# Expert layers of a two-block network: routing weights from one product per token, with GpSimd taking part

## The reference, cut to what matters

```
s = einsum('thpk,pnk->thpn', q, sub_keys); s_top, i_top = top_k(s, 16)
cand = s_top[:, :, 0, :, None] + s_top[:, :, 1, None, :]
g_top, pos = top_k(cand, 16); expert = i_top0 * 128 + i_top1 at pos
g = softmax(g_top)
act = gelu(einsum('thkd,td->thk', u[expert], x))
out = einsum('thk,thkd->td', g * act, v[expert])
```

## Time and profile before

| what | value |
|---|---|
| median of 3 runs | 2693.94 us |
| lowest and highest run | 2690.03 and 2698.76 us |
| span of the profiled execution | 2688.2 us |
| expert layers' up tiles with routing steps | about 401.6 to 663 and 1401 to 1663 us |
| granted clock of PE in these stretches | 1.00 |

### The profile page before, as it was taken

The page is one execution under the profiler, slowest core; times in us unless marked ns, Lnnn a source line. Parts: engine busy times, 40 slices in busy tenths (PEclk is TensorE's granted clock), DMA queues, the critical chain, the costliest instruction groups (busy, mean ns, idle before and its releaser), DMA issues.

```text
span 2688.2 us, 48883 instructions
## 1 busy us (share of the span) xinstructions
PE 2605.5 (97%) x17304; PEld 2387.0 (89%) x17304; DVE 1996.2 (74%) x3791; ACT 1506.0 (56%) x2602; POOL 346.1 (13%) x190
## 2 busy tenths in 40 slices
PE   6999999999999999999999999999999999998998
PEld 6779999999888888889999999888888889887997
DVE  6768957888887876669867888666666686677766
ACT  4455557766565556555557766665554544463443
POOL 4007600000000002617500000000000101002000
PEclk9999999999999999999999999999999999999999
DMA  6844564444788874424664444555555345442553
GB/s 243 282 137 164 197 228 149 142 143 148 266 279 272 280 264 145 149 94 167 204 213 143 148 142 150 195 191 192 195 187 187 108 176 188 165 164 96 187 188 133
DMA packets 134733, 490.88 MB, mean 183 GB/s; under 512 B 15520, under 2 KB 15608, under 8 KB 134288
## 3 DMA queue, kind: packets, MB, share of 16 engines
q1 hardware_dynamic: 131904, 480.31, 52.6%
q0 software_dynamic: 2640, 8.02, 0.9%
HBM read 487.21 MB, written 1.06 MB: 182 GB/s over the span
## 4 chain that ended last, share of the span: by engine, by line
PE 87%; DVE 6%; ACT 2%; DMA 2%; issue 1%; POOL 0%; SPq 0%; DVEq 0%; ACTq 0%
PE ps L224 78%; PE ps L1308 4%; DMA weight_ring<-in_stream 2%; ACT weight_split L239 1%; PE ps L641 1%; DVE weight_split L248 1%; DVE arena L633 1%; ACT arena L396 1%; PE ps L2473 1%; PE ps L1280 1%; POOL weight_split L248 0%; DVE arena L1909 0%; PE ps L389 0%; DVE arena L1913 0%; PE ps L662 0%
## 5 line engine op out<-in xcount | busy, mean ns | idle before, releaser
L224 PE MATMUL ps<-hT_split,weight_split 128*128 128x256 f32 x9792 | 1234.3, 285 | 9.8 <-DVE hT_split L421 4.6
L224 PEld LDWEIGHTS ps<-hT_split,weight_split 128*128 128x128 f32 x9792 | 1196.2, 192 | 20.1 <-issue 13.8
L248 DVE TENSOR_TENSOR weight_split<-weight_ring,weight_split 128x1024 fp32r<-128x1024 f32 x674 | 823.5, 1223 | 403.0 <-ACT weight_split L239 400.4
L239 ACT ACTIVATE weight_split<-weight_ring 128x1024 fp32r<-128x1024 f32 x800 | 848.2, 1061 | 259.7 <-PE ps L224 167.8
L224 PE MATMUL ps<-weight_split,hidden_split 128*128 128x512 f32 x3948 | 914.8, 391 | 7.6 <-DVE hidden_split L1574 4.0
L224 PEld LDWEIGHTS ps<-weight_split,hidden_split 128*128 128x128 f32 x3948 | 736.4, 188 | 160.9 <-issue 8.0
L248 POOL TENSOR_TENSOR weight_split<-weight_ring,weight_split 128x1024 fp32r<-128x1024 f32 x126 | 306.2, 2433 | 410.5 <-ACT weight_split L239 410.2
L1404 ACT ACTIVATE hidden_split<-arena 128x256 fp32r<-128x256 f32 (+1 forms) x256 | 176.3, 689 | 249.0 <-PE ps L224 248.5
L1396 ACT ACTIVATE arena<-ps 128x256 f32<-128x256 f32 (+18 forms) x248 | 126.9, 512 | 133.5 <-PE ps L224 133.5
L224 PE MATMUL ps<-weight_split,hT_split 128*128 128x512 f32 x660 | 159.1, 396 | 9.0 <-DVE weight_split L248 4.7
L1574 DVE TENSOR_TENSOR hidden_split<-arena,hidden_split 128x256 fp32r<-128x256 f32 x256 | 161.2, 630 | 0.0
(11 more groups left out here) (357 smaller groups left out, 1765.7 us busy)
## 6 DMA issues: line engine op xcount, KB each, us to landing
weight_ring<-in_stream SPq DMA_DIRECT2D x912, 512.0 KB, 3.3
x<-in_x SPq DMA_DIRECT2D x1, 1024.0 KB, 5.0
arena<-mlstm_m_rows POOLq DMA_DIRECT2D x1, 1024.0 KB, 6.7
arena<-in_ln_mix_g POOLq DMA_DIRECT2D x2, 512.0 KB, 4.8
arena<-in_ln_mix_b POOLq DMA_DIRECT2D x2, 512.0 KB, 6.2
arena<-in_ln_ffn_g POOLq DMA_DIRECT2D x2, 512.0 KB, 4.6
arena<-in_ln_ffn_b POOLq DMA_DIRECT2D x2, 512.0 KB, 6.3
out<-x SPq DMA_DIRECT2D x2, 512.0 KB, 2.6
```

The costliest lines, as they stand in the source:

```text
L224: mm = pe.matmul(out_, stationary(s_part), moving(m_part), start=start and n == 0, stop=stop and n == 2, skip_group_check=True)
L239: act.activation(wsplit[:, n % SPLITS, HIGH, :], ring[:, slot(POS[n]), :], ACT.Copy).then_inc(high_ready, 1)
L248: eng.tensor_tensor(w[:, REST, :], ring[:, slot(POS[n]), :], w[:, HIGH, :].bitcast(fp32), ALU.subtract).then_inc(split_ready, 1)
```

## The change

The four one-hots of a step are shared out anew, and PE gets another product:
- POOL `places_i` makes the four plain one-hots of i (no weight), as fp32r, one instruction a token, two steps ahead. Its first two steps wait for the columns and for the last use of the buffer (mod_ready).
- The weights g are split once a layer into HIGH and REST (`pr_gain`, ACT and DVE `gains_rest`). DVE `places_j` makes for every token a pair of one-hots of j, one weighted by HIGH, one by REST: one instruction of 2x128 elements with two SBUF tensors and one scalar, two tokens at a time, into six slots.
- PE takes one fp32r product of 128x256 a token: the plain one-hot stationary, the pair moving. The two halves of the result, in two pairs of PSUM banks, have to be added.
- ACT `high_out` copies the HIGH halves of a step (512 elements) to SBUF (`pr_w`). DVE `summed` adds the REST halves: the weights of done tiles into `pr_w`, those of later tiles into `acts_late`.
- POOL `weigh` multiplies the activations of done tiles by `pr_w`, all in SBUF.
- ACT's `keep` and `places_j`, DVE's `places_i` and `weigh` are gone.
- The scratch space of software transfers is set to 8192.

The diff, cut to its core:

```diff
+        pr_gain = sbuf("routing_gains_split", [128, 2, T], fp32r)
+        pr_w = sbuf("routing_weights", [128, 2, 4, 128])
...
+            def places_i(q):
+                if q >= 2:
+                    pool.wait_ge(pr_built, STEPS * l + q - 1)
+                for a in range(STEP):
+                    step = pool.tensor_scalar(pr_ohi[:, q % 2, a], iota[:], pr_cols[:, 0, STEP * q + a:STEP * q + a + 1], None, ALU.is_equal)
+                step.then_inc(pr_ohi_r, 1)
+
+            def weigh(q):
+                w, tokens = pr_w[:, q % 2], slice(STEP * q, STEP * q + STEP)
+                pool.wait_ge(pr_summed, STEPS * l + q + 1)
+                pool.wait_ge(activated_ready, 128 * l + STEP_AT[q])
+                early, late = acts_early[:, tokens, :], acts_late[:, tokens, 0:STEP_AT[q] - EARLY]
+                pool.tensor_tensor(early, early, w[:, :, 0:EARLY], ALU.mult)
+                pool.tensor_tensor(late, late, w[:, :, EARLY:STEP_AT[q]], ALU.mult).then_inc(pr_routed, 1)
+
+            pool.wait_ge(pr_cols_out, 2 * (l + 1))
+            pool.wait_ge(mod_ready, 14 if l else 6)
+            places_i(0)
+            places_i(1)
+            for q in range(STEPS):
+                weigh(q)
+                if q + 2 < STEPS:
+                    places_i(q + 2)
...
             def routing(q):
                 pe.wait_ge(pr_ohi_r, STEPS * l + q + 1)
+                pe.wait_ge(pr_ohj_r, 2 * (STEPS * l + q + 1))
+                if q >= 2:
+                    pe.wait_ge(pr_summed, STEPS * l + q - 1)
                 for a in range(STEP):
-                    mm = pe.matmul(ps[:, q % 3, 128 * a:128 * a + 128], pr_ohi[:, q % 2, a, :], pr_ohj[:, q % 3, a, :].bitcast(fp32),
-                                   start=True, stop=True)
+                    mm = pe.matmul(ps[:, 2 * (q % 2) + a // 2, 256 * (a % 2):256 * (a % 2) + 256], pr_ohi[:, q % 2, a, :],
+                                   pr_ohj[:, (STEP * q + a) % J_SLOTS].rearrange("p k j -> p (k j)"), start=True, stop=True)
...
+            def high_out(q):
+                act.wait_ge(pr_built, STEPS * l + q + 1)
+                if q >= 2:
+                    act.wait_ge(pr_routed, STEPS * l + q - 1)
+                    act.wait_ge(pr_kept, STEPS * l + q - 1)
+                act.activation(pr_w[:, q % 2], step_weights(q, HIGH), ACT.Copy).then_inc(pr_high_out, 1)
...
             for j in range(128):
                 if j - 1 in STEP_AT:
-                    keep(with_step(j - 1))
-                if j + 1 in STEP_AT:
-                    places_j(with_step(j + 1))
+                    high_out(with_step(j - 1))
...
+            def summed(q):
+                w, low, tokens = pr_w[:, q % 2], step_weights(q, REST), slice(STEP * q, STEP * q + STEP)
+                dve.wait_ge(pr_high_out, STEPS * l + q + 1)
+                dve.tensor_tensor(w[:, :, 0:STEP_AT[q]], low[:, :, 0:STEP_AT[q]], w[:, :, 0:STEP_AT[q]], ALU.add).then_inc(pr_summed, 1)
+                dve.tensor_tensor(acts_late[:, tokens, STEP_AT[q] - EARLY:], low[:, :, STEP_AT[q]:], w[:, :, STEP_AT[q]:], ALU.add).then_inc(pr_kept, 1)
...
+            def places_j(q, pair):
+                n = q - 1 + pair
+                if n >= 1:
+                    dve.wait_ge(pr_built, STEPS * l + n)
+                for a in (2 * pair, 2 * pair + 1):
+                    t = STEP * q + a
+                    step = dve.scalar_tensor_tensor(out=pr_ohj[:, t % J_SLOTS], in0=iotas(2), scalar=pr_cols[:, 1, t:t + 1],
+                                                    in1=pr_gain[:, :, t:t + 1].bitcast(fp32).broadcast_to([128, 2, 128]), op0=ALU.is_equal, op1=ALU.mult)
+                step.then_inc(pr_ohj_r, 1)
...
             for j in range(HEAD, 129):
-                if j - 1 in STEP_AT:
-                    weigh(with_step(j - 1))
+                if j in STEP_AT:
+                    places_j(with_step(j), 1)
                 if j + 1 in STEP_AT:
                     if with_step(j + 1) == 0:
-                        dve.wait_ge(pr_cols_out, 2 * (l + 1))
-                    places_i(with_step(j + 1))
+                        gains_rest()
+                    places_j(with_step(j + 1), 0)
                 if j + 2 < 131:
                     up_rest(j + 2)
                 if j == FIRST_STEP - 2:
                     mod_out_dve(row, 7)
+                if j - 1 in STEP_AT:
+                    summed(with_step(j - 1))
                 if j - 1 >= FIRST_STEP:
                     weigh_tile(j - 1)
-                if j + 1 in STEP_AT:
-                    places_j(with_step(j + 1))
```

More of the change, by code:

```diff
@@ L126, in build @@
             pass
+        with nc.sbuf_tensor("below_places", [128, ROUTE + 768], fp32), nc.sbuf_tensor("places_i", [128, 2, 4, 128], fp32r) as pr_ohi:
+            pass
         arena = sbuf("arena", [128, EDGE])
+        pr_gain = sbuf("routing_gains_split", [128, 2, T], fp32r)
+        pr_w = sbuf("routing_weights", [128, 2, 4, 128])
         ps = ctx.enter_context(nc.psum_tensor("ps", [128, 8, 512], fp32))
@@ L1225, in build, with step_weights @@
         pr_sum = pr(2, TB * 8)
-        pr_cols = edge_a.rearrange("p (n t) -> p n t", n=3)
-        STEP, ACT_J = 4, 2
+        pr_cols = edge_a[:, 0:2 * T].rearrange("p (n t) -> p n t", n=2)
+        STEP, J_SLOTS = 4, 6
         STEPS = T // STEP
         assert len(STEP_AT) == STEPS and EARLY < FIRST_STEP
-        pr_ohi = edge_b.rearrange("p (n a i) -> p n a i", n=2, a=STEP)
-        pr_ohj = hidden[:].rearrange("p n a t -> p (n a t)").rearrange("p (n a i) -> p n a i", n=3, a=STEP)
+        pr_ohj = hidden[:].rearrange("p n a t -> p (n a t)").rearrange("p (n k j) -> p n k j", n=J_SLOTS, k=2)
         (pr_par, pr_q_out, pr_scored, pr_s_out, pr_topped, pr_chosen, pr_exp_in, pr_exp, pr_cols_t, pr_cols_out,
-         pr_ohi_r, pr_distance, pr_ohj_act, pr_ohj_dve, pr_built, pr_routed, pr_kept, pr_weighted) = (sem("peer_" + s) for s in (
+         pr_gain_r, pr_ohi_r, pr_ohj_r, pr_built, pr_high_out, pr_summed, pr_routed, pr_kept, pr_weighted) = (sem("peer_" + s) for s in (
              "params_in", "q_out", "scored", "scores_out", "topped", "chosen", "exp_in_ready", "exp_ready", "cols_turned", "cols_out",
-             "onehots_i_ready", "places_distance_ready", "onehots_j_act_ready", "onehots_j_dve_ready", "routing_built", "done_tiles_weighted",
+             "gains_split", "onehots_i_ready", "onehots_j_pair_ready", "routing_built", "routing_high_out", "routing_summed", "done_tiles_weighted",
              "routing_kept", "tile_weighted"))
-        def step_weights(q):
-            return ps[:, q % 3, :].rearrange("p (a j) -> p a j", a=STEP)
+        def step_weights(q, part):
+            b = 2 * (q % 2)
+            return ps[:, b:b + 2, :].rearrange("p b (a k j) -> p (b a) k j", a=2, k=2)[:, :, part, :]
         def with_step(j):
@@ L1409, in hidden_first @@
                 hidden_top(j)
-            def keep(q):
-                act.wait_ge(pr_routed, STEPS * l + q + 1)
-                act.activation(acts_late[:, STEP * q:STEP * q + STEP, STEP_AT[q] - EARLY:], step_weights(q)[:, :, STEP_AT[q]:], ACT.Copy).then_inc(pr_kept, 1)
-            def places_j(q):
-                if q >= 3:
-                    act.wait_ge(pr_built, STEPS * l + q - 2)
-                for a in range(ACT_J):
-                    step = act.activation(pr_ohj[:, q % 3, a, :], iota[:], ACT.Abs, scale=-1.0, bias=pr_cols[:, 1, STEP * q + a:STEP * q + a + 1])
-                step.then_inc(pr_distance, 1)
-                act.wait_ge(pr_distance, STEPS * l + q + 1)
-                near = pr_ohj[:, q % 3, 0:ACT_J]
-                act.activation(near, near.bitcast(fp32), ACT.Relu, scale=-1.0, bias=1.0).then_inc(pr_ohj_act, 1)
+            def high_out(q):
[4 more added lines that the diff above has]
+                act.activation(pr_w[:, q % 2], step_weights(q, HIGH), ACT.Copy).then_inc(pr_high_out, 1)
             def exps():
@@ L1536, in up_rest, with gains_rest @@
                     ada_dve((104 if l else 40) + (j - HEAD) // 2, edge_b)
-            def weigh(q):
-                g, tokens = step_weights(q), slice(STEP * q, STEP * q + STEP)
-                dve.wait_ge(pr_built, STEPS * l + q + 1)
-                dve.wait_ge(activated_ready, 128 * l + STEP_AT[q])
-                early, late = acts_early[:, tokens, :], acts_late[:, tokens, 0:STEP_AT[q] - EARLY]
-                dve.tensor_tensor(early, early, g[:, :, 0:EARLY], ALU.mult)
-                dve.tensor_tensor(late, late, g[:, :, EARLY:STEP_AT[q]], ALU.mult).then_inc(pr_routed, 1)
+            def gains_rest():
+                dve.wait_ge(pr_cols_out, 2 * (l + 1))
+                dve.tensor_tensor(pr_gain[:, REST, :], ps[:, 3, 0:T], pr_gain[:, HIGH, :].bitcast(fp32), ALU.subtract).then_inc(pr_gain_r, 1)
+                dve.wait_ge(pr_gain_r, l + 1)
+            def summed(q):
[3 more added lines that the diff above has]
```

(1 more changed line is left out.)

22 lines of the change are left out of this document (3 added, 19 removed).

## The result

The changed kernel takes 2799.56 us (median, 2797.47 to 2801.51) against 2691.99 us of the kernel before beside it: a ratio of 1.0404, 95% interval 1.0387 to 1.0422, about 108 us **slower**. The sign was forecast and the time lies inside the stated range, but the forecast of 33 us more is a third of what came.

A forecast was written before the change was run, and what follows sets the result against it. PE bounds the routing stretch before; after, DVE with POOL's turns: 3.70 + 0.53 = 4.23 us a step, a group 31.0 against 29.2, over 18.3 groups 33 us more, 2727 us. Range of 8 in 10: 2650 to 2840.

The forecast's parts named there:

- the term of 0.53 us a step: In DVE's step tile: POOL's 2.50 us less 0.97 beside PSUM reads and 1.00 of hidden start-up leaves 0.53 added.
- POOL alone would fit within 3.36: POOL's work in a routing step, 2.50 us, low end 1.62, was to fit within PE's step tile of 3.36 us.
- PE: Routing product on PE falls from 0.88 to 0.48 us, a step tile from 3.76 to 3.36; 51 us if PE stayed the bound.
- ACT: ACT in the routing stretch loses work and gains one 512-element PSUM copy, up to 1.06 us: nothing on the path.
- DVE's list: DVE's work in a step tile without POOL: 1.13 + 4 x 0.40 + 0.68 + 0.29 = 3.70 us, a group 27.3.
- two instructions with 512 elements together make 0.68: DVE's two sums of a step: 0.08 us fixed each and 1.02 ns an element, together 0.68 us.
- second case: PE and DVE alone count, POOL's small instructions slipping in between DVE's: 34 us less, 2660 us; chance 0.27.
- POOL's price: POOL's four one-hots at 0.38 us each plus two weighing products at 0.98 us: 2.50 us a step.
- The weighing: POOL's two products of a step, mean 352 elements together: 0.82 to 0.98 us, 0.98 taken.
- Taking turns: DVE instructions reading two SBUF tensors and POOL's reading SBUF exclude each other: 33 us more, 2727 us; chance 0.53.
- My sum with DVE as the bound: DVE's step tile 3.70 + 0.53 = 4.23 us, its group 31.0 us against PE's 29.2 before: 33 us more.
- third case: Turns without hidden start-ups, or POOL dearer than its one row says: 161 us more, 2855 us; chance 0.20.

The follow-up runs named there:

- first experiment: Changed kernel with POOL's one-hots of i one element wide from the third step on and both weighing products one element each: 2686.08 us, ratio 0.9982.
- third experiment: Changed kernel with DVE's pairs reading the numbers from PSUM and its REST parts subtracting a PSUM bank (wrong values), so no shared reads: 2692.51 us, ratio 1.0001.
- the edit of 2: Changed kernel with the row of numbers copied once a layer to PSUM, so DVE's pairs read only one SBUF tensor: 2734.96 us, ratio 1.0154.

## Why the prediction was right or wrong

The forecast was 33 us more, the result 108. **The step that failed is the term of 0.53 us a step, POOL's time put into DVE's list, with POOL's own waiting put at nothing ("POOL alone would fit within 3.36").** In its place the runs show POOL as the bound: a list of 3.3 us a step without company, and on top about 1.2 us of waiting for its turn on average; in the step shown both make 4.83 us. The parts, one by one:

- **PE: right.** Where PE had to wait, it is 562.66 - 562.09 = 0.57 us from the start of the four passes to the next tile's products; where it had not, 0.47, and step tiles follow each other by 3.35 us (first experiment: routing products at 403.12 and 406.47, the tile's own at 403.59), as worked out. The gain of 0.40 us a step was real and could not be collected.
- **ACT: right.** It is busy for 107.3 us of the stretch, and the sum waits for its copy for 3.5 us in all (DVE L1565).
- **DVE's list: too short by 0.18 us a step.** The term that is off is "two instructions with 512 elements together make 0.68"; it is 0.86 (third experiment), and the 0.18 is a wait that the change adds and that I did not see, 0.10 of it between the two records: `weigh_tile` now waits for a sum of its own engine that stands right in front of it, where ACT's copy had been early. The pairs (0.39 against 0.40) were right. With 3.88 a group takes 7 x 3.88 + 1.42 = 28.6 us against 29.2: the case without turns is about 11 us less, and not 34. The first experiment gave 6 us less, the third no difference; the two halves of its REST part make 0.06 us a step, 8 us, of that. A slip in the prediction's second case, 24.9 for what is 27.3 - 8 x 0.29 = 25.0, is worth 1 to 2 us.
- **POOL's price: too low by 0.8 us a step.** "A one-hot: 0.20 us by the memset's line, 0.38 by the product's. I take 0.38." It is 0.58 start to start. The product's line was drawn through one point, with the memset's fixed part; the fixed part of this instruction is 0.28. The weighing was nearer (0.98 forecast, 1.0 to 1.1 measured). What the prediction calls a product of 1024 on POOL is the subtraction of L248; the true products are shorter in their fixed part than the one-hots, 0.19 us with one element in the first experiment (L1288, median 191 ns). POOL's own list is 4 x 0.58 + 1.0 = 3.3 us a step, not 2.50.
- **Taking turns: right as a mechanism, wrong in who pays.** I put POOL's time into DVE's list and let POOL keep its own price. In fact DVE lost 554 - 477 = 77 ns on a pair, 0.3 us a step, and POOL 906 - 603 = 303 ns on a one-hot, 1.2 us a step. With a list of its own of 3.3 us that makes POOL's 4.5 to 5 us the pace, and PE waits for one-hots rather than for split tiles, as I had said. My sum with DVE as the bound (4.23 us a step) gave a third of the loss. Price and waiting were both needed: the third experiment has the full price and no loss, and a list of 2.50 with 1.2 of waiting would take 3.7 us (an estimate), less than DVE's 3.88 and 0.3.
- **The range held in part by luck.** With the measured prices in it the same sum reads 3.32 - 0.97 - 1.00 = 1.35 us a step, DVE's tile 3.88 + 1.35 = 5.23 and a group 38.0 against 29.2: 161 us more, too much by half. Prices that were too low and the wrong engine made up for each other in part.
- **The rivals.** The second case, that small instructions would slip in between, is refuted by the third experiment beside the changed kernel. Granted clock and loss do not go together: with the edit of 2 the clock over the run is 0.992, within the 0.990 to 0.997 of the kernel before, and 43 us of the loss are still there. The third case named two causes; the first, start-ups that are not hidden, was not tested by itself; of the second, "POOL dearer than its one row says" and "the loop through POOL" are what happened, through turns that POOL pays, at 2800 and not 2855 us. I gave it 0.20 and should have kept both ends of the one-hot's price open.
- **The rule on shared reads.** The Trainium skill (SBUF — State Buffer, Who interferes with whom) says that a GpSimd instruction that reads SBUF meets every DVE instruction with two SBUF inputs. The runs agree: with one operand moved to PSUM the pairs fell from 554 to 477 ns. They agree for instructions as short as 0.28 us too: the one-hots of one element took 546 ns on average in the first experiment. The Trainium skill (GPSIMD Engine Reference, Elementwise — side-by-side cycle accounting) gives its 4497 ns for an addition of two tensors, which I took for a product; my estimate from it was a fixed part of 0.30 us, and 1.32 us for the weighing. The one-element one-hot measured 0.28, so for this instruction that was better than my 0.09 from the memsets; a one-element product measured 0.19, between the two, and the weighing of 348 elements took 0.54 + 0.46 = 1.00 us, nearer to my 0.98.

## What to carry to other kernels

Before work goes to GpSimd beside a busy VectorE, count in VectorE's list the instructions that read two SBUF tensors, and see whether one of the two can be read from PSUM: here that single operand was worth 65 us. Price a GpSimd instruction with a fixed part per instruction, and count the waits for turns on both engines: here GpSimd paid 1.2 us a step on its one-hots and VectorE 0.3 on its pairs. An instruction that waits for the one right in front of it on its own engine is worth moving a place back, behind other work; here that gave 8 and 13 us, together with what the earlier sum gave POOL. Not tried: POOL's one-hots ahead of its weighing, which would let them go without waiting for DVE's sum.

## What the runs showed of the hardware that was not expected

- GpSimd's comparison with a column (128 elements, fp32 to fp32r) takes 592 ns alone and 277 with one element, while its memset of 256 takes 309: the elements cost 2.5 ns each, where the memset's cost 0.9 and those of two-tensor instructions 2.2 (587 ns for 204 elements, 2399 for 1024).
- The shares of waiting are unequal: with six shared instructions a step on GpSimd's side and five on VectorE's, GpSimd's one-hots lengthen by a half (603 to 906 ns) and VectorE's pairs by a sixth (477 to 554).
- PE's granted clock falls to the lower of its two levels, 1.2 GHz, for parts of the stretch, where it was 1.00 over all of it before. Windows of the changed kernel, two of 20 us and one of 2 us inside the second, with the columns of the earlier trace rows:

```profile
400.00:420.00 20.00, 16.21 (x134) 15.80 (x132) 17.58 (x37) 10.97 (x21) 16.50 (x23) 1.00 0.40 132
420.00:440.00 20.00, 15.52 (x107) 15.31 (x108) 13.29 (x26) 6.25 (x12) 16.57 (x26) 0.83 0.31 106
434.00:436.00 2.00, 2.00 (x11) 2.00 (x11) 1.90 (x5) 0.00 (x0) 2.00 (x4) 0.50 0.00 0
```

PE was busy for 81% of the first of these. The clock fell during a wait of 3.6 us for one-hots that ended at 431.46: it was 1.00 over 428 to 430 us and 0.53 over 430 to 432. At 0.50 PE shows 11 products of 128x256 in 2 us, against 19 in 2 us at 1.00. How much of the 108 us this took was not tried by itself; in the run without turns the clock over the whole run is back at 0.993, from 0.987.
